# How many pieces of the next head's preparation go to each halt of a gated delta rule

## What is computed

```python
def gdn_mixer(qkv, z, ab, conv_w, a_log, dt_bias, norm_g):
    qkv = jax.nn.silu(centred_dwconv(qkv, conv_w)).astype(F32)     # 5 taps
    q, k, v = jnp.split(qkv, [HA * DKA, 2 * HA * DKA], axis=-1)
    q = l2norm(q.reshape(B, S, HA, DKA)) * (DKA ** -0.5)
    k = l2norm(k.reshape(B, S, HA, DKA))
    ...
    o_f = gated_delta_chunked(qh, kh, vh, gh[:, 0], bh[:, 0])
    o_b = flip(gated_delta_chunked(flip(qh), flip(kh), flip(vh), flip(gh[:, 1]), flip(bh[:, 1])))
    o = rmsnorm(o_f + o_b, norm_g) * jax.nn.silu(z)
```

## Time and profile before

| | us |
|---|---|
| three runs | 4160.53, 4170.31, 4163.24 |
| median | 4163.24 |
| profiled execution, its own time | 4159.45 |
| its span, first to last instruction | 4157.7 |

### The profile page before, as it was taken

One profiled execution on the slowest core, in us unless ns is written; L12 is line 12 of the kernel. 1 busy time (PEld: TensorE's weight loads), 2 busy tenths in 40 slices (PEclk: granted clock), 3 DMA queues, 4 the chain that ended last, 5 costly groups with the idle time before them and its releaser, 6 DMA issues. The chain is left out here.

```text
span 4157.7 us, 48483 instructions
## 1 busy us (share of the span) xinstructions
PE 3544.2 (85%) x17648; PEld 2902.6 (70%) x17648; DVE 2308.1 (56%) x4342; ACT 1375.3 (33%) x2570; POOL 579.7 (14%) x450
## 2 busy tenths in 40 slices
PE   7787788778689999778878999889998779788997
PEld 6666666666568888557756888668887557576886
DVE  3555634656338875567663333347875667653333
ACT  3313333133323333333433232233332334424321
POOL 1000010000103332111111110103332100102100
PEclk9988899888899999889989999999999889899999
DMA  4531035311243221212333333342222212323332
GB/s 126 149 107 34 18 103 143 112 34 31 61 140 105 77 73 55 70 57 79 82 89 91 91 96 86 107 138 76 82 63 83 59 51 62 106 84 88 95 96 66
DMA packets 553874, 350.06 MB, mean 84 GB/s; under 512 B 73220, under 2 KB 497156, under 8 KB 553372
## 3 DMA queue, kind: packets, MB, share of 16 engines
q1 hardware_dynamic: 553628, 346.84, 29.3%
HBM read 301.36 MB, written 45.42 MB: 83 GB/s over the span
## 5 line engine op out<-in xcount | busy, mean ns | idle before, releaser
L658 PE MATMUL bank<-h,w_hi 128*128 128x512 f32 (+1 forms) x1728 | 761.2, 441 | 187.0 <-DVE w_low L651 158.4
L659 PE MATMUL bank<-h,w_hi 128*128 128x512 f32 (+1 forms) x1728 | 707.1, 409 | 0.0
L660 PE MATMUL bank<-h,w_low 128*128 128x512 f32 (+1 forms) x1728 | 707.1, 409 | 0.0
L658 PEld LDWEIGHTS bank<-h,w_hi 128*128 128x128 f32 (+1 forms) x1728 | 344.4, 199 | 285.0 <-DVE w_low L651 170.0
L645 ACT CAST w_hi<-w 128x1024 fp32r<-128x1024 f32 (+1 forms) x328 | 298.9, 913 | 456.9 <-DMA w<-in_w_in 295.4
L651 DVE TENSOR_TENSOR w_low<-w,w_hi 128x1024 fp32r<-128x1024 f32 (+1 forms) x328 | 372.2, 1136 | 77.8 <-ACT w_hi L645 72.8
L660 PEld LDWEIGHTS bank<-h,w_low 128*128 128x128 f32 (+1 forms) x1728 | 341.6, 198 | 82.3
L659 PEld LDWEIGHTS bank<-h,w_hi 128*128 128x128 f32 (+1 forms) x1728 | 345.1, 200 | 72.3 <-issue 9.6
L459 DVE TENSOR_TENSOR w_low<-w,w_hi 128x1024 fp32r<-128x1024 f32 x128 | 174.6, 1364 | 155.4 <-ACT w_hi L453 155.4
L1300 ACT ACTIVATE prob<-bank,softmax_stat 128x512 f32<-128x512 f32 (+3 forms) x256 | 145.2, 568 | 289.8 <-DVE softmax_stat L1332 224.8
L659 PE MATMUL bank<-yT_low,w_hi 128*128 128x512 f32 x512 | 215.6, 421 | 0.0
(11 more groups left out here) (435 smaller groups left out, 7152.8 us busy)
## 6 DMA issues: line engine op xcount, KB each, us to landing
w<-in_w_in SPq DMA_DIRECT2D x148, 512.0 KB, 4.2
w<-in_w_mlp SPq DMA_DIRECT2D x128, 512.0 KB, 4.0
z<-z_tile SPq DMA_DIRECT2D x164, 256.0 KB, 4.1
w<-in_w_gate SPq DMA_DIRECT2D x64, 512.0 KB, 4.1
q_twice<-z SPq DMA_DIRECT2D x128, 128.0 KB, 3.2
w<-in_w_branch SPq DMA_DIRECT2D x64, 256.0 KB, 2.9
k_twice<-z SPq DMA_DIRECT2D x88, 128.0 KB, 3.7
w<-in_w_out SPq DMA_DIRECT2D x32, 256.0 KB, 2.8
```

Of the source, the lines that this page charges most:

```text
L658: self.t.matmul(bank[0:n, :], wh, high, start=j == 0, stop=False)
L659: self.t.matmul(bank[0:n, :], wh, low, start=False, stop=False)
L660: return self.t.matmul(bank[0:n, :], wl, high, start=False, stop=j == self.depth(i) - 1)
```

## The change

One table is changed. Every piece keeps its content and its order on its engine.

```diff
-    AHEAD = (0, 0, 0) + (2,) * 12 + (2,) + (1,) * 8 + (1, 1)
+    AHEAD = (0, 0, 1) + (1,) * 12 + (1,) + (2,) * 8 + (2, 2)
```

## The result

The change makes the kernel slower: 4212.81 us (median of five runs, 4203.88 to 4214.87) against 4164.96 us for the kernel before in the same comparison. The ratio is 1.010, with a 95% interval of 1.0081 to 1.0120. The difference is 48 us, where 24 us was forecast, and the time lies above the forecast's range (4169 to 4204 us). The profiled execution took 4214.87 us with a span of 4213.1 us, against 4159.45 and 4157.7 us before.

What follows compares the result with a forecast made beforehand. TensorE was taken to set the pace except at the levels' small waits and the head's end. Levels -3.5, scan 0, end +23.5, clock +5, w_low -2, with handoffs +24 us: 4187 us, range 4169 to 4204 us.

Steps and rivals of the forecast that it cites:

- the end: At each head's end, TensorE's second l2 product waits for ScalarE's square of k behind the output's chain: +23.5 us.
- the waits: TensorE's waits at the heads' ends: 21.0 us a pass against 9.3 us, an increase of 23.5 us in all.
- the clock: Behind the end-of-head waits, the clock falls to half in all six hand-overs: +5 us, ends 0 and +10.
- handoffs: At each of the six waits at the hand-overs, 0.2 us for the handoff.
- The Trainium skill's rule on table sets: ScalarE at heads' ends: one load for Ln and Exp would make the increase 16 us in place of 23.5.
- The levels: In the levels, two pieces in place of four shorten TensorE's waits for M: -3.5 us, ends 0 and 5.9 us.
- The scan: In the scan over chunks, TensorE's stream halt covers seven more VectorE operations: 0 us.
- Rival A: The scan turns VectorE-bound as well: 32 us on top, 4219 us, half of that likelier (4203 us); chance 0.13.
- rival B: In the levels, VectorE's queue is the true brake and emptying half makes the kernel faster: 4149 us; chance 0.07.
- C: No change: waits at the heads' ends grow by under 1.5 us a head, about 4165 us; chance 0.09.
- the last sentence on the clock: At the second and sixth heads' starts, VectorE starts earlier relative to TensorE, shrinking w_low waits: -2 us, ends 0 and -4.

Runs made afterwards that it cites:

- experiment 1: Kernel before with only the last six pieces of a preparation late, at halts 23 to 25 as in the change; 4210.86 us, ratio 1.009.
- run 9: Kernel before with fewer pieces in the levels and one stream halt of each head moved from the levels to halt 24; 4158.83 us, ratio 0.9982.
- run 10: Kernel before, its table of pieces kept, with two stream halts of each head moved from the levels to halt 24; 4144.82 us, ratio 0.9955.
- Experiment 3: Changed kernel with both l2 squares in one ScalarE piece at halt 23, ahead of the output's chain; 4182.37 us, ratio 1.0029.
- experiment 4: Kernel before with five extra chained copies of q_now on VectorE at each head's start, ahead of the decays; 4189.48 us, ratio 1.0045.
- experiment 6: Changed kernel with GpSimd's first level mask held until VectorE's second M is made; 4194.57 us, ratio 1.0070.
- experiment 2: Kernel before with only pieces 33 and 34 (second l2's Ln, Exp and scaling) late, at halt 25; 4176.64 us, ratio 1.0016.

## Why the prediction was wrong

**The direction, the place and the mechanism of the end were right.** From the last o product to the next head's first product, six hand-overs took 68.0 us before and 107.2 us after, 39.1 us more. Of that, 8.6 us are work that left the stretch in front of it (the l2 products, U to the last o product), so the net is 30.6 us. The forecast had 23.5 for the waits, 5 for the clock and 1 for handoffs, 29.5 us. The waits of L2625 were forecast at 21.0 us a pass and are 20.8 us; with L2803's, TensorE waits 48.2 us at the heads' ends against 25.2 us, 23.0 us more.

**The clock, right.** All six hand-overs have their stretch at 1.2 GHz, as forecast. The two windows are those behind the second and third waits; the clock stands in the third column from the end:

```profile
1485.20:1493.90 8.70, 8.61 (x33) 6.15 (x34) 4.59 (x13) 5.13 (x7) 0.61 (x1) 0.76 0.00 1
1592.80:1602.20 9.40, 9.30 (x32) 6.64 (x33) 2.97 (x9) 4.17 (x6) 0.61 (x1) 0.69 0.11 31
```

Their loss is 8.7 x 0.24 = 2.1 us and 9.4 x 0.31 = 2.9 us; summed so over the six it is 14.5 us, where 15 us was forecast, and 4.5 us more than before's 10 us.

**The Trainium skill's rule on table sets.** "ScalarE: Activation LUTs", section "Table sets: the hidden batching unit", would have had one load for Ln and Exp. After the change, too, a load of 1.28 us stands ahead of each of them (1478.50 above is Exp's). The measurement decides: the waits are 20.8 us a pass, and an estimate by the page's rule, one load for a pair, is 21.0 - 7.7 = 13.3 us.

**The levels, right in four heads.** In the first, second, fifth and sixth heads they fell by 5.1 us together (3.5 forecast, 5.9 as the far end), and the stage of experiment 1 gives the relief 5.9 us.

**The scan, right.** The first scan takes 14.5 us against 15.5, the second 13.4 us against 14.1, and TensorE waits in it for nothing that counts. Rival A, VectorE as the bound of the scan, did not come. Rivals B and C did not either. (The nine VectorE operations that come into the scan, pieces 15 to 26, are five convolutions and four of the gates, not six and three; the sum does not change.)

**The step that failed is the last sentence on the clock**: "With TensorE slow and VectorE not, VectorE starts the next head earlier relative to it", with its -2 us for w_low in the second and sixth heads, ends 0 and -4. It has the wrong sign. In the second and sixth heads the first wait for w_low went from 1.0 to 1.4 us, and what counts lies in the third and seventh heads, which the prediction left alone. VectorE's lead at the start of the third and seventh heads was 2.97 and 1.99 us before and is 0.62 us in both after. Two things took it, and the rows show both:
- The lead came from the slow clock, but from the part of it that lies **behind** L2803. VectorE's copy (L2947) waits for L2803, so what counts is how long TensorE takes from there to its first product of the head: 5.2 us at half clock in the second hand-over before, 2.9 us now, because a longer wait *ahead of* L2625 has moved the half-clock stretch forward and the clock is full again at L2803. A stretch that I counted as an ally of VectorE had moved to the wrong side of the hand-over.
- The last l2 operation (L2698, 0.68 us) now stands between that copy and the decays. I had traced this operation to TensorE, who needs its result, and found it in time; I had not asked what it delays on its own engine.

The other runs give the sizes. Runs 9 and 10 have full clock at these hand-overs and no L2698 in the way: lead 1.01 to 1.02 us, wait for w_low 4.0 us. Experiment 3 has L2698 (L2699 there) in the way and half clock: lead 2.36 and 2.23 us, wait 4.0 us. So the clock took 2.0 and 1.0 us of the lead and L2698 the last 0.4 us, and neither alone would have brought the long wait; the change has both.

With the lead gone, VectorE's low half and its second pair for M fall behind GpSimd's operations. The wait for w_low at the third and seventh heads grows from 4.0 to 8.2 us, and a stretch at half clock stands behind it; these two heads' levels lost 5.5 and 4.2 us, and the fourth and eighth, whose lead fell from 1.65 and 1.88 to 0.02 us, lost 2.1 us each for MT (L2891). Together 13.9 us against the -2 us forecast. The sum is then closed: 30.6 - 5.1 + 13.9 = 39.4 of the stage's 40.5 us.

Experiments 3, 4 and 6 take this apart: without the wait ahead of L2625 the lead and the old w_low wait come back; with VectorE held back and the table of before the 8.2 us wait appears; and with GpSimd's mask held back it falls to 4.0 us at the same lead, 2.9 us of it by VectorE's faster pair. The price of the lost lead was also outside the range that I had set: the ends 0 and -4 had no end on the losing side, though the profile showed 46.98 of 48.50 us busy on VectorE and a convolution at 1.14 or 0.77 us depending on its company. The Trainium skill, "SBUF — State Buffer", section "Who interferes with whom", which I used only for rival B, describes the same meeting as a shared port pair; experiment 6 agrees with it, with 1.79 us for 0.68 us.

**What stays open.** The 40.5 us of the stage leave 7 us of the medians' 48 us. The kernel before has medians of 4164.21 to 4168.89 us in the three sets of the experiments, which would make the difference 44 to 49 us, so part of these 7 us can be the scatter of before's own medians. The first meeting with GpSimd, at 1496.98, was not taken away by itself, and the fourth and eighth heads' 2.1 us each are read from the waits and from experiments 2 and 6. No experiment was made on the rest.

## What to carry over

A moved wait has to be priced on every queue that it reaches: not only who waits for it, but who was running ahead of the waiting engine, and by how much. Engines that share a resource are kept apart by such leads; write down the smallest one at each meeting, and give the term an end on the losing side when it is small. And where a stage waits at one place while its cover is spread evenly over all of it, moving cover to that place is worth trying ahead of moving work away from a busy engine: here it gave 0.5%, where the relief of the levels gave some 6 us by the stage at most and nothing by itself.

## What the runs showed of the hardware

A delay of 0.4 us on VectorE (lead 1.02 against 0.62 us) went with 4.2 us more waiting on TensorE. 128x512 operations with both inputs in SBUF take 0.69 us alone and 1.4 to 1.8 us when a GpSimd operation on such inputs is already under way, and each slowed one pushes the next into the same company. Which of the two starts first matters: L2872 at 1486.18, 0.03 us ahead of GpSimd's L2961, kept its 0.69 us, and the same operation at 1499.14, behind it, took 1.79 us.

The half-clock stretches begin in a wait of TensorE or shortly behind it, and end while it works on: the one at the second hand-over before covers all of 1478.10 to 1483.20, and after the change the stream products are back at 0.39 us from 1489.56 on, 4.3 us behind the end of the wait. Which part of the program they cover goes by where the wait stands, so a longer wait can leave the work *after* it at a higher clock: 2.9 us from L2803 to the next head in all six hand-overs after the change, and 2.8 to 5.2 us before.

Identical instructions don't take identical time. All kernels here have the same program up to the first delta rule. The windows from the start to its beginning, for the kernel before and then after (4380 matmuls, 1353 VectorE and 694 ScalarE operations in each):

```profile
0.00:1094.70 1094.70, 868.51 (x4380) 711.73 (x4380) 591.28 (x1353) 326.35 (x694) 56.64 (x46) 0.87 0.29 83
...
0.00:1100.50 1100.50, 875.36 (x4380) 714.03 (x4380) 591.31 (x1353) 326.09 (x694) 56.30 (x46) 0.86 0.30 82
```

VectorE and ScalarE are busy equally long, TensorE is not: 868.51 and 875.36 us at clocks of 0.87 and 0.86. Over the twelve kernels this point lies between 1094.0 and 1108.6 us. One profile's total is thus uncertain by more than most single terms of a forecast like this, and the stage that is touched is the place to compare.
